# Transforming the Hyena filters by token classes mod 4, with the sums on PoolE

## The reference

```
def hyena_mixer(h, w_in, conv_w, conv_b, f_w1, ..., z, decay):
    u = dwconv3(h @ w_in, conv_w, conv_b)
    v, x1, x2 = jnp.split(u, 3, axis=-1)
    a = ...                                  # a small MLP of the position
    filt = (a @ f_w3).reshape(L, HY_ORDER, 2, D) * decay[:, None, None, :]
    fwd, bwd = filt[:, :, 0], filt[:, :, 1]
    k2 = jnp.concatenate([fwd, jnp.zeros_like(fwd[:1]), bwd[1:][::-1]], axis=0)
    k2 = k2 / jnp.sum(jnp.abs(k2), axis=0, keepdims=True)
    kf = jnp.fft.rfft(k2, axis=0)
    zc = v
    for o in range(HY_ORDER):                # 2
        zf = jnp.fft.rfft(zc, n=2 * L, axis=1)
        y = jnp.fft.irfft(zf * kf[None, :, o], n=2 * L, axis=1)[:, :L]
        zc = gates[o] * (y + skip[o] * zc)   # gates = (x1, x2)
    return zc @ w_out
```

## Time and profile before

| | us |
|---|---|
| median of 3 runs | 3034.92 (3033.46 to 3039.18) |
| profiled execution, its time | 3032.25 |
| profiled execution, span | 3030.4 |
| mean granted clock of TensorE | 0.968 of full |
| the convolution, from k(0,0) to the first product with hy_w_out | 2365.2 to 2594.1 |

### The profile page before, as it was taken

The page is one execution under the profiler, slowest core; times in us unless marked ns, Lnnn a source line. Parts: engine busy times, 40 slices in busy tenths (PEclk is TensorE's granted clock), DMA queues, the critical chain, the costliest instruction groups (busy, mean ns, idle before and its releaser), DMA issues.

```text
span 3030.4 us, 40334 instructions
## 1 busy us (share of the span) xinstructions
PE 2858.6 (94%) x15683; PEld 2296.0 (76%) x15683; DVE 1324.4 (44%) x1917; ACT 702.0 (23%) x1076; POOL 1608.7 (53%) x1569
## 2 busy tenths in 40 slices
PE   7998998999989999999989999999989998899998
PEld 6998887789768877888865567888867465788886
DVE  5676654311350275334344634331167677433312
ACT  2275223532330001111014532110011222211100
POOL 5652214655136665666652136766576443676663
PEclk9998999999999999999999999999999999999999
DMA  3221000222002455565531013333222100233331
GB/s 111 83 63 41 2 2 29 83 70 70 28 17 96 153 168 178 182 194 184 193 122 50 15 42 84 97 97 106 88 89 84 49 18 14 84 84 97 102 96 66
DMA packets 291842, 259.82 MB, mean 86 GB/s; under 512 B 6538, under 2 KB 264183, under 8 KB 291437
## 3 DMA queue, kind: packets, MB, share of 16 engines
q1 hardware_dynamic: 287840, 248.53, 26.3%
q0 software_dynamic: 2416, 6.34, 0.7%
q10 hardware_dynamic: 1436, 2.96, 0.3%
HBM read 255.72 MB, written 2.10 MB: 85 GB/s over the span
## 4 chain that ended last, share of the span: by engine, by line
PE 78%; DVE 10%; issue 5%; DVEq 2%; ACT 2%; POOL 1%; DMA 1%; POOLq 0%; ACTq 0%; SPq 0%
PE ps L509 21%; PE ps L511 21%; PE ps L510 21%; DVE cv L2102 2%; PE ps L1581 1%; PE ps L1426 1%; PE ps L1561 1%; DVE HS L646 1%; PE ps L1416 1%; DVE HSL L639 1%; PE ps L1406 1%; PE ps L1546 1%; PE ps L1182 1%; PE ps L1493 1%; PE ps L1168 1%
## 5 line engine op out<-in xcount | busy, mean ns | idle before, releaser
L713 POOL CAST spl<-raw 128x512 fp32r<-128x512 f32 (+1 forms) x352 | 248.8, 707 | 721.2 <-PE ps L511 566.0
L509 PE MATMUL ps<-HSH,spl 128*128 128x512 f32 x1344 | 540.1, 402 | 40.6 <-DVE HSL L639 19.4
L715 POOL TENSOR_TENSOR spl<-raw,spl 128x512 fp32r<-128x512 f32 (+1 forms) x352 | 500.6, 1422 | 60.4 <-issue 10.6
L510 PE MATMUL ps<-HSL,spl 128*128 128x512 f32 x1344 | 530.0, 394 | 0.0
L511 PE MATMUL ps<-HSH,spl 128*128 128x512 f32 x1344 | 529.7, 394 | 0.0
L719 POOL TENSOR_TENSOR spl<-raw,spl 128x512 fp32r<-128x512 f32 (+1 forms) x352 | 479.6, 1362 | 51.8 <-issue 1.8
L509 PE MATMUL ps<-HNH,spl 128*128 128x264 f32 (+1 forms) x1152 | 370.0, 321 | 26.1 <-DVE HNL L641 6.0
L510 PE MATMUL ps<-HNL,spl 128*128 128x264 f32 (+1 forms) x1152 | 361.1, 313 | 0.0
L511 PE MATMUL ps<-HNH,spl 128*128 128x264 f32 (+1 forms) x1152 | 360.1, 313 | 0.0
L509 PEld LDWEIGHTS ps<-HSH,spl 128*128 128x128 f32 x1344 | 256.1, 191 | 121.2 <-issue 44.3
L717 POOL CAST spl<-raw 128x512 fp32r<-128x512 f32 (+1 forms) x352 | 229.6, 652 | 211.1 <-PE ps L511 208.9
(11 more groups left out here) (435 smaller groups left out, 4471.7 us busy)
## 6 DMA issues: line engine op xcount, KB each, us to landing
adw<-in_ada_w SPq DMA_DIRECT2D x96, 512.0 KB, 5.5
raw<-in_w_in SPq DMA_DIRECT2D x44, 1024.0 KB, 5.2
raw<-in_ffn_w_up SPq DMA_DIRECT2D x88, 512.0 KB, 4.8
raw<-in_w_ffn_in SPq DMA_DIRECT2D x44, 512.0 KB, 5.0
raw<-in_ffn_w_down SPq DMA_DIRECT2D x16, 1408.0 KB, 6.5
raw<-in_hy_w_in SPq DMA_DIRECT2D x12, 1024.0 KB, 5.2
raw<-in_w_ffn_out SPq DMA_DIRECT2D x8, 1408.0 KB, 6.8
raw<-in_w_branch_dn SPq DMA_DIRECT2D x8, 1024.0 KB, 5.1
```

What stands on the lines that cost most here:

```text
L509: pe.matmul(dst, w[0], x[0], start=first, stop=False)
L510: pe.matmul(dst, w[0], x[1], start=False, stop=False)
L713: pool.tensor_copy(hi[:, first, :], w[:, first, :])
L715: pool.tensor_tensor(lo[:, first, :], w[:, first, :], hi[:, first, :], ALU.subtract).then_inc(split_first, 1)
```

## The change

The filters' tokens are now ordered by classes mod 4: tokens 0, 2, 1, 3 mod 4 stand in the four tiles (by_class in the tables, of_class in the program). The second block of frequencies is written in reverse, 255 - f, for signal and inverse too. At frequency 255 - f the cosine and the sine of an even token are, up to sign and exchange, those at f, and the sign depends on the class alone. So k_transform(u, even) does 4 products (two classes, cosine and sine, first block only), one in each bank, and k_transform(u, odd) does 8 (two blocks, two classes).

PoolE takes k_even(u): four sums and differences, two into KP[0] and two into a place that is free at that time (even_rest: a part of the tile square and a part of raw). Then k_odd(u): four that combine KP[0] with the odd products, then y_kp; and four more into KP[1], then y_kp again. That is 12 instructions for a unit where there were 8. k_out now waits for y_kr, which a drain of PoolE counts behind k_even and behind k_odd. KP[0] is there only after k_odd's first half, so multiply(0,0) is given a function that it calls between its two parts: filter_out(1, 0 and 1) and filter_sum(1, 0 and 1) now stand ahead of its wait for y_kp.

```diff
-    f = np.arange(SEQ // 2)
+    f = np.concatenate([np.arange(P), SEQ // 2 - 1 - np.arange(P)])
+    by_class = np.concatenate([t[0::4], t[2::4], t[1::4], t[3::4]])
...
-            def k_parts(u, f):
-                pool.wait_ge(y_kc, 2 * u + f + 1)
+            def k_even(u):
+                pool.wait_ge(y_kc, 2 * u + 1)
                 if u:
-                    pool.wait_ge(y_cb, 4 * (u - 1) + 2 * f + 2)
-                ce, co, se, so = (KS[:, n, :] for n in range(4))
-                pool.tensor_tensor(KP[:, f, 0, :], ce, co, ALU.add)
-                pool.tensor_tensor(KP[:, f, 1, :], se, so, ALU.add)
-                pool.tensor_tensor(KP[:, f, 2, :], ce, co, ALU.subtract)
-                pool.tensor_tensor(KP[:, f, 3, :], so, se, ALU.subtract).then_inc(y_kp, 1)
+                    pool.wait_ge(y_cb, 4 * (u - 1) + 2)
+                c0, c2, s0, s2 = (KS[:, n, :] for n in range(4))
+                pool.tensor_tensor(KP[:, 0, 0, :], c0, c2, ALU.add)
+                pool.tensor_tensor(KP[:, 0, 1, :], s0, s2, ALU.add)
+                pool.tensor_tensor(even_rest[0], c0, c2, ALU.subtract)
+                pool.tensor_tensor(even_rest[1], s2, s0, ALU.subtract)
+                pool.drain().then_inc(y_kr, 1)
+            def k_odd(u):
+                pool.wait_ge(y_kc, 2 * u + 2)
+                oc, os, oc_rest, os_rest = (KS[:, n, :] for n in range(4))
+                pool.tensor_tensor(KP[:, 0, 2, :], KP[:, 0, 0, :], oc, ALU.subtract)
...
+                pool.tensor_tensor(KP[:, 0, 1, :], KP[:, 0, 1, :], os, ALU.add).then_inc(y_kp, 1)
+                if u:
+                    pool.wait_ge(y_cb, 4 * u)
+                pool.tensor_tensor(KP[:, 1, 0, :], even_rest[0], oc_rest, ALU.add)
...
+                pool.tensor_tensor(KP[:, 1, 3, :], os_rest, even_rest[1], ALU.subtract).then_inc(y_kp, 1)
+                pool.drain().then_inc(y_kr, 1)
...
             for u in range(UNITS):
                 if u:
                     y_parts(u, 0)
                 if u + 1 < UNITS:
-                    k_parts(u + 1, 0)
+                    k_even(u + 1)
                 y_parts(u, 1)
                 if u + 1 < UNITS:
-                    k_parts(u + 1, 1)
+                    k_odd(u + 1)
...
-                for s in range(2):
-                    for t in range(NT):
-                        mm = pe.matmul(ps[:, s * 2 + t // 2, :], t_fwd[:, s, t, fs], PM[:, s, t, :],
-                                       start=t % 2 == 0, stop=t % 2 == 1)
+                if odd:
+                    for f in range(2):
+                        for s in range(2):
+                            for t in range(2):
+                                mm = pe.matmul(ps[:, 2 * f + s, :], t_fwd[:, s, 2 + t, f * P:(f + 1) * P], PM[:, s, 2 + t, :],
+                                               start=t == 0, stop=t == 1)
+                else:
+                    for s in range(2):
+                        for t in range(2):
+                            mm = pe.matmul(ps[:, 2 * s + t, :], t_fwd[:, s, t, 0:P], PM[:, s, t, :], start=True, stop=True)
...
             def k_out(u, f):
                 act.wait_ge(y_k, 2 * u + f + 1)
                 if u or f:
-                    act.wait_ge(y_kp, 2 * u + f)
+                    act.wait_ge(y_kr, 2 * u + f)
...
-            def multiply(u, f):
+            def multiply(u, f, between=None):
...
                 dve.drain()
+                if between:
+                    between()
                 dve.wait_ge(y_kp, 2 * u + f + 1)
...
-            multiply(0, 0)
-            filter_out(1, 0, 0)
-            filter_out(1, 1, 2)
-            filter_sum(1, 0)
-            filter_sum(1, 1)
+            def next_filters():
+                filter_out(1, 0, 0)
+                filter_out(1, 1, 2)
+                filter_sum(1, 0)
+                filter_sum(1, 1)
+
+            multiply(0, 0, next_filters)
```

More of the change, by code:

```diff
@@ L101, in tables @@
     rope = flat([np.tile(np.cos(ang), (2, 1)), np.tile(np.sin(ang), (2, 1))])
-    f = np.arange(SEQ // 2)
+    f = np.concatenate([np.arange(P), SEQ // 2 - 1 - np.arange(P)])
     w = np.pi * ((2 * f[:, None] + 1) * t[None, :] % (4 * SEQ)) / (2 * SEQ)
     by_parity = np.concatenate([t[0::2], t[1::2]])
+    by_class = np.concatenate([t[0::4], t[2::4], t[1::4], t[3::4]])
     rows = lambda a: flat([a[n * P:(n + 1) * P] for n in range(len(a) // P)])
-    fwd = flat([rows(np.cos(w).T[by_parity]), rows(np.sin(w).T[by_parity])])
+    fwd = flat([rows(np.cos(w).T[by_class]), rows(np.sin(w).T[by_class])])
     inv_dft = flat([rows(np.cos(w)[:, by_parity] / SEQ), rows(np.sin(w)[:, by_parity] / SEQ)])
@@ L117, in tables @@
     deltas = np.abs(np.linspace(np.log(1e-2) / 1.5, np.log(1e-2) / 0.3, D, dtype=np.float32))
-    decay = np.exp(-lin * deltas[None, :]).astype(np.float32)[by_parity]
+    decay = np.exp(-lin * deltas[None, :]).astype(np.float32)[by_class]
     return {"t_square": flat(square), "t_delta": flat(delta), "t_rope": rope, "t_fwd": fwd,
@@ L399, in build @@
         y_conv, y_f, y_ab, y_pm, y_n, y_rn = sem("y_conv"), sem("y_f"), sem("y_ab"), sem("y_pm"), sem("y_n"), sem("y_rn")
-        y_t, y_tc, y_k, y_kc, y_kp = sem("y_t"), sem("y_tc"), sem("y_k"), sem("y_kc"), sem("y_kp")
+        y_t, y_tc, y_k, y_kc, y_kr, y_kp = sem("y_t"), sem("y_tc"), sem("y_k"), sem("y_kc"), sem("y_kr"), sem("y_kp")
         y_dft, y_zc, y_x, y_cb, y_y, y_inv, y_z = sem("y_dft"), sem("y_zc"), sem("y_x"), sem("y_cb"), sem("y_y"), sem("y_inv"), sem("y_z")
@@ L568, in build @@
         t_fwd = at("t_fwd", [2, NT, SEQ // 2], hy_in.slot(10) * SLOT)
+        even_rest = [square[:, P:P + SEQ], raw[:, 0, 2 * NT * SEQ // 2:2 * NT * SEQ // 2 + SEQ]]
         t_inv = at("t_inv", [2, 2, SEQ], hy_in.slot(11) * SLOT)
@@ L1000, in _ @@
             filter_in(1)
-            k_parts(0, 0)
-            k_parts(0, 1)
+            k_even(0)
+            k_odd(0)
             y_parts(0, 0)
@@ L1484, in _ @@
             pe.matmul(ps[0:FW, 7, :], W1[:, :], POS[:, :], start=True, stop=True).then_inc(y_mlp, 1)
-            even_odd = lambda x, n: x.rearrange("p (h i e) -> p e h i", e=2, h=2)[:, n // 2, n % 2, :]
+            of_class = lambda x, n: x.rearrange("p (q r) -> p r q", r=4)[:, (0, 2, 1, 3)[n], :]
             def filter_tile(u, t, b):
@@ L1492, in filter_tile @@
                 for s in range(2):
-                    mm = pe.matmul(ps[:, b + s, :], even_odd(A1[:, 1 - s, :], t), W3[:, :], start=True, stop=True)
+                    mm = pe.matmul(ps[:, b + s, :], of_class(A1[:, 1 - s, :], t), W3[:, :], start=True, stop=True)
                 mm.then_inc(y_f, 1)
@@ L1530, in turn_in, with k_transform @@
                     for c in range(NT):
-                        mm = pe.transpose(ps[:, 4 + t % 2, c * P:(c + 1) * P], even_odd(U[:, u % 2 * NT + c, :], t), ident)
+                        mm = pe.transpose(ps[:, 4 + t % 2, c * P:(c + 1) * P], of_class(U[:, u % 2 * NT + c, :], t), ident)
                     mm.then_inc(y_t, 1)
-            def k_transform(u, f):
-                if f:
+            def k_transform(u, odd):
+                if odd:
                     pe.wait_ge(y_kc, 2 * u + 1)
```

6 lines of the change are left out of this document (5 added, 1 removed).

## The result

The changed kernel takes 3044.45 us (median of 11 runs, 3041.22 to 3047.53), the kernel before 3033.61 us in the same comparison (11 runs, 3028.20 to 3039.18). The ratio is 1.0034, 95% interval 1.0025 to 1.0043: slower, by 10.8 us. The forecast was 3046.2 us with a range of 3039 to 3052. The profiled execution took 3041.22 us, its span is 3039.4 us.

What follows compares the result with a forecast made beforehand. TensorE is 94% busy, but the chain through VectorE and PoolE decides. Terms 4.0 + (6.6 - 4.0) + 2.1 + 1.0 + 1.0 + 0.6 = +11.3 us gave 3046.2 us, range 3039 to 3052.

Steps and rivals of the forecast that it cites:

- That the removed products don't pay: Four of 16 products per unit, 13.7 us if all on the path; in units 2 and 3 only idle time.
- Rival A: Faster, 3028 us: k(0,0) and k(1,0) each save 3.43 us on the chain and VectorE keeps up; chance 0.06.
- k(1,0), +4.0 forecast: Unit 0: VectorE's multiply(0,0) comes later, so k(1,0) starts at 2408.2 instead of 2404.20, +4.0 us.
- meeting: A PoolE sum beside a VectorE instruction with two SBUF inputs: the pair takes 1.67 us, costing VectorE up to 1.07.
- filter_norm(1), +6.6 forecast: Unit 1: the filter's sums on VectorE end at 2428.4, before 2421.9, so filter_norm(1) waits and comes 6.6 us later.
- The clock behind it, +2.1 forecast: Behind the wait at filter_norm(1) TensorE loses 3.0 us to the clock, 0.9 of it idle before: +2.1 us.
- Into units 2 and 3, +1.0 each forecast: At the transposes TensorE stands 6 us instead of 3.3 and loses 3 instead of 2 us to the clock: +1.0 each.
- Unit 3 and the end, +0.6 forecast: The sums of k_odd(3) reach into unit 3's multiplication, where there was none before: +0.6 us.
- The drain, 0 forecast: PoolE's drain that counts y_kr, ahead of k_out(2,1) and k_out(3,1): bounds 0 to 2.4 us in all, taken as 0.
- rival C: Slower still, 3050 to 3056 us: drains cost a sum each, pairs meet oftener, late sums reach filter_norm inside z(u,0); chance 0.15.
- the four waits: TensorE stands about 10 us ahead of k(1,0), 4 to 5 ahead of filter_norm(1), about 6 at units 2 and 3's transposes.
- Rival B: No change that can be told, 3037 to 3040 us: filter's absolute-value sums in time, clock lost once; chance 0.11.

Runs made afterwards that it cites:

- experiment 4: Changed kernel with k_even's four products done twice, so TensorE has 16 products per unit again; 3044.30 us, ratio 1.0031.
- experiment 1: Kernel before with 4 of the 8 filter products of block 0 left out per unit, nothing added; 3036.64 us, ratio 1.0011.
- experiment 11: Kernel before with 4 of 8 block 0 filter products left out and PoolE's first sums of unit 1 held until multiply(0,1) is done; 3031.82 us.
- experiment 8: Changed kernel with unread products keeping TensorE busy in its waits (filter_norm(1), transposes of units 2 and 3, last inverse); 3043.47 us, ratio 1.0034.
- experiment 9: Changed kernel with PoolE's first sums of unit 1, k_even(1), held until multiply(0,1) is done; 3039.92 us, ratio 1.0024.
- experiment 10: Kernel before with only the filter work moved between multiply(0,0)'s XZ and its products; 3037.71 us, ratio 1.0018.
- experiment 3: Changed kernel with the filter work of unit 1 put back behind the whole of multiply(0,0); 3048.88 us, ratio 1.0052.
- 2: Kernel before with four more PoolE sums per unit, results not read, all 16 products kept; 3036.48 us, ratio 1.0014.
- 6 to 9: 6: kernel before, transposes' copies ahead of k_out(u+1,1) in units 2 and 3, 3031.26 us; 7: kernel before, unread products in TensorE's waits, 3029.41 us.
- experiment 5: Change in units 2 and 3 only, units 0 and 1 as in the kernel before except for k_parts' drain; 3037.84 us, ratio 1.0015.
- 12: Kernel before with transposes' copies first in units 2 and 3, plus two unread products ahead of unit 3's filter tiles and inverse(2); 3031.26 us.

## Why the prediction was right, point by point

**That the removed products don't pay.** Right, and shown: put back, they cost nothing (experiment 4), taken out alone they give nothing (1 and 11), within intervals of some 3 to 4 us to either side. They lay where TensorE waits for VectorE or PoolE a moment later. Rival A falls with it: k(1,0) starts 4.5 us later, not earlier.

**k(1,0), +4.0 forecast, +4.5 measured.** Right for the reason given, that multiply(0,0) comes later, but parts of the working were off. I held KP[0] for the last thing that the products wait for; it was ready at 2385.9, and VectorE began them at 2392.68, when it was through with the filter work, 31.0 behind k(0,0) instead of the 29.5 of my working. The filter tiles took 5.52 us, not 3.71, after the same idle 1.97 us. That is not what made the start late, though: in experiments 8 and 9, with the same program up to here and tiles of 3.82 us, it is 30.7. There the three filter sums all met PoolE (1.69, 1.73 and 1.60 us in experiment 8) and took 6.3 us, for which I had 5.2. One meeting fewer in multiply(0,0) (two, not three) gave 0.9 back. What sets the start is the filter work, and its tiles wait for the copy of k(0,1); experiment 10 shows it without any late KP.

**filter_norm(1), +6.6 forecast, +8.6 measured.** The step of the largest error, 2 us. The forecast had k_even(1) reach the last two instructions of multiply(0,1), and it reached four: TensorE stood 8.55 us and k(1,0) lost 2.0 us to the clock, not 3.0, so its copy started at 2410.92, while multiply(0,1) was as late as k(1,0). That cost two more meetings of 1.07. Experiment 8 went the way of the forecast: a wait of 9.93 us, 3.2 lost to the clock, two instructions caught, the sums ready 6.2 us later than before. The two runs have the same program up to there and part at the filter tiles, 5.52 us in one and 3.82 in the other. So the 2 us are not a cost of the change that every execution must pay; how often each way is taken isn't shown, and the forecast had no term for it. The meeting itself was a mechanism of the forecast, and experiment 11 shows it by its removal from experiment 1, with equal filter tiles in both: 4.0 us at filter_norm(1), 3.6 of length.

The price of a meeting was as the rows before had it: in the kernel after, two of the caught instructions start 1.67 us apart (2413.31 and 2414.98 above), as in the earlier trace rows. The Trainium skill, "SBUF — State Buffer", Who interferes with whom, has the second of the two fully blocked, which would make it 1.82; the trace does not bear out that size, though the direction is right.

**The clock behind it, +2.1 forecast, +1.9 measured** (10.5 less 8.6). Right, with two errors that cancel: the term was 3.0 lost less 0.9 of idle time between the transposes before. That idle time was 0.48 us in TensorE's timeline (at 2424.59), and the loss then comes to 2.4. The granted clock in the stretches behind the waits was 0.50, the lower of its two levels, in these windows of the trace after:

```profile
2405.50:2408.00 2.50, 2.50 (x3) 0.97 (x4) 2.40 (x4) 0.00 (x0) 1.83 (x3) 0.50 0.34 103
2427.50:2430.00 2.50, 2.50 (x13) 2.50 (x14) 0.18 (x1) 0.00 (x0) 2.50 (x3) 0.50 0.00 0
2488.50:2490.50 2.00, 2.00 (x3) 0.81 (x3) 2.00 (x3) 1.82 (x3) 1.30 (x1) 0.50 0.00 0
```

(PEclk is the third figure from the end.)

**Into units 2 and 3, +1.0 each forecast, +0.8 and about +0.1 measured.** The waits became 6.00 and 5.73 us, as forecast, but the clock came back sooner than I had taken from the inverse's 9.85 us: behind the first the transposes took 1.98 us for 1.70 and the filter tiles 8.40 for 8.23, which with 0.3 of the drain is the 0.8; behind the second z(3,0) took 8.73. A term mis-sized by 1.1 us in all: I had carried over what a longer wait cost in another place.

**Unit 3 and the end, +0.6 forecast, −0.5 measured** (10.9 less 11.4). The last wait for XZ grew from 5.88 to 6.84 us (+1.0), as the sums of k_odd(3) suggested, but the second half of the inverse then ran in 7.17 instead of 8.64 us and gave 1.5 back. I had not seen that a term at the very end can turn round by the clock.

**The drain, 0 forecast.** The gap between PoolE's last sum and the copy grew by 0.3 us in unit 2 and 0.06 in unit 3 (0.15 for 0.09): near the end of the bounds that I chose, and far from rival C's 1.22 each.

So the total came out within half a microsecond (11.3 for 10.9 in the profile and 10.8 in the medians) with errors that cancel: 1.8 us too little up to z(1,0) (8.7 for 10.5), 2.2 too much behind it (2.6 for 0.4). The chain and the places of the four waits were right; that the sum came so close is luck. The working also has slips that change nothing: multiply(0,0) is given 10.8 us where its terms give 7.8 + 3 x 1.07 = 11.0 (the 2408.2 has it right), multiply(0,1) 9.7 for 9.9, 2428.4 less 2421.9 is 6.5 and not 6.6, and the chances of the cases add up to 0.09 for no change and 0.08 for faster, not 0.10 and 0.07. Rival B, that the sums of the filter are in time, would have needed PoolE out of multiply(0,1), and experiment 9, which does just that, lands at 3039.92 us, in B's band. What stays open is how the 10.8 us split between edits: sums alone, the move alone and products alone lose 3.8, 5.0 and 4.0 us in their medians, but they all go through the same place in unit 1, so they can't be added, and the 6.8 us of length that the move saves in experiment 3 have the other sign.

## What to carry to other kernels

When an engine that is 94% busy waits for others inside a stage, take its products out alone before building anything in their place: here 13.7 us of them were worth nothing that the runs can tell, and the change that removed them lost 10.8. An engine that becomes early can start a third one beside a second, and slow that down. Then look at what stands beside the instructions that will now start sooner, and try one wait that holds them back. And read what follows each new idle stretch at the clock that the engine had there, each place by itself.

## What the runs showed of the hardware that was not expected

- After the same idle 1.97 us, the same eight records of filter tiles took 3.7 to 3.8 us in the profiled executions of nine kernels (before, experiments 1, 2, 4, 6 to 9 and 11) and 5.4 to 5.5 us in five (after, experiments 3, 5, 10 and 12), with a granted clock of 1.00 before and 0.70 and 0.77 in after and experiment 5, in windows of 1.6 to 2 us at their start. Each kernel was profiled once, so whether this belongs to the kernel or to the execution is open. TensorE's code ahead of these tiles is the same in the kernel before and in experiments 10 and 12, and the whole program ahead of them is the same in the kernel after (5.52) and in experiments 8 and 9 (3.82), which speaks for the execution.
- Where that clock fell with the old order of the filter work (experiments 5 and 12), k(1,0) was not slow: the wait there had shrunk from 2.41 to 1.38 us, and it took 7.13 us instead of 8.83. The quicker k(1,0) then made filter_norm(1) wait 4.5 us, and z(1,0) came 4.6 and 4.3 us later than before. A quicker k(1,0) made what follows slower by 4 us, by way of PoolE's earlier sums beside VectorE's.
